# A mixture-of-experts stage: padding rows skipped, the residual gathered and added on VectorE, experts of different groups in turn

## What is computed

```
gi   = argmax(x @ w_rg + b_rg)              # one of 4 groups for each token
le   = (x @ w_re[gi] + b_re[gi])            # 8 experts in the group
top_p, top_i = top_k(softmax(le), 2)        # two of them, both of the same group
gate = p_top * top_p / sum(top_p)
# (token, expert) pairs sorted by expert, each expert padded to blocks of 128 rows
hid  = silu(xb @ w_gate[e]) * (xb @ w_up[e])      # 1024 -> 256
y[token] += gate * (hid @ w_down[e])              # 256 -> 1024
h = h + y
```

## Time and profile before

| | us |
|---|---|
| median of 3 runs | 3121.38 |
| lowest, highest | 3119.2, 3127.32 |
| profiled execution | 3119.75 |
| its span | 3117.8 |

### The profile page before, as it was taken

One profiled execution on the slowest core, in us unless ns is written; L12 is line 12 of the kernel. 1 busy time (PEld: TensorE's weight loads), 2 busy tenths in 40 slices (PEclk: granted clock), 3 DMA queues, 4 the chain that ended last, 5 costly groups with the idle time before them and its releaser, 6 DMA issues. The chain is left out here.

```text
span 3117.8 us, 48627 instructions
## 1 busy us (share of the span) xinstructions
PE 2673.4 (86%) x15109; PEld 2236.8 (72%) x15112; DVE 1747.1 (56%) x3154; ACT 1260.4 (40%) x2369; POOL 724.0 (23%) x923
## 2 busy tenths in 40 slices
PE   5999979997968947998898599799879947989997
PEld 4999958875847836777676488578658836767775
DVE  4222246665755665667765366588733354676664
ACT  3222132225841104556654222288611104675653
POOL 1000023321110002444343143211100002444433
PEclk9999989998988968999999799899979968999998
DMA  6111112215536516899997322222154415999995
GB/s 243 50 56 52 40 60 78 75 65 165 163 121 234 194 61 216 261 301 302 316 281 228 118 87 80 91 83 88 53 198 143 149 39 179 298 359 285 283 308 132
DMA packets 175389, 509.57 MB, mean 163 GB/s; under 512 B 53800, under 2 KB 81456, under 8 KB 150320
## 3 DMA queue, kind: packets, MB, share of 16 engines
q1 hardware_dynamic: 142480, 393.69, 34.7%
q0 software_dynamic: 32800, 114.51, 15.4%
HBM read 374.56 MB, written 133.56 MB: 163 GB/s over the span
## 5 line engine op out<-in xcount | busy, mean ns | idle before, releaser
L1700 DVE TENSOR_TENSOR moe_parts<-expert_w,moe_parts 128x1024 fp32r<-128x1024 f32 x384 | 452.3, 1221 | 238.4 <-ACT moe_parts L1649 234.9
L1582 PE MATMUL ps<-moe_parts,moe_xT 128*128 128x512 f32 x2232 | 551.6, 403 | 23.0 <-issue 16.0
L1582 PEld LDWEIGHTS ps<-moe_parts,moe_xT 128*128 128x128 f32 x2232 | 418.1, 191 | 125.3 <-issue 20.5
L1649 ACT ACTIVATE moe_parts<-expert_w 128x1024 fp32r<-128x1024 f32 x384 | 373.3, 1047 | 80.3 <-PEq L155 78.8
L1109 PE MATMUL ps<-out_w,out_catT 128*128 128x512 f32 x1344 | 322.4, 399 | 14.2 <-DVE out_w L1265 11.8
L560 PE MATMUL ps<-in_gate_w,in_gate_hnT 128*128 128x384 f32 (+1 forms) x1536 | 319.4, 367 | 7.4 <-DVE in_gate_w L679 7.4
L1582 PE MATMUL ps<-moe_parts,moe_hidT 128*128 128x512 f32 x1116 | 289.0, 408 | 26.9 <-DVE moe_hidT L1713 24.2
L560 PEld LDWEIGHTS ps<-in_gate_w,in_gate_hnT 128*128 128x128 f32 x1536 | 278.7, 190 | 37.4 <-issue 7.5
L1109 PEld LDWEIGHTS ps<-out_w,out_catT 128*128 128x128 f32 x1344 | 255.7, 192 | 69.4 <-DVE out_w L1265 12.6
L560 PE MATMUL ps<-in_qk_w,in_qk_hnT 128*128 128x512 f32 x1152 | 268.4, 394 | 9.2 <-DVE in_qk_w L679 9.2
L1582 PEld LDWEIGHTS ps<-moe_parts,moe_hidT 128*128 128x128 f32 x1116 | 205.7, 191 | 76.2 <-DVE moe_hidT L1713 32.8
(11 more groups left out here) (262 smaller groups left out, 4150.8 us busy)
## 6 DMA issues: line engine op xcount, KB each, us to landing
expert_w<-in_w_gate SPq DMA_DIRECT2D x64, 1024.0 KB
expert_w<-in_w_up SPq DMA_DIRECT2D x64, 1024.0 KB
expert_w<-in_w_down SPq DMA_DIRECT2D x64, 1024.0 KB
hn_d<-out_hn SPq DMA_DIRECT2D x32, 512.0 KB, 2.6
in_gate_xt<-in_x SPq DMA_DIRECT2D x16, 512.0 KB
in_qk_xt<-in_x SPq DMA_DIRECT2D x16, 512.0 KB
att_k<-k_d SPq DMA_DIRECT2D x64, 128.0 KB, 2.9
out_ht<-in_x SPq DMA_DIRECT2D x16, 512.0 KB, 4.6
```

The lines of the kernel that those rows point to most:

```text
L1582: last = nc.tensor.matmul(out, left[:, a, k, :], right(b, k), start=(n == 0 and k == 0), stop=(n == 2 and k == K_ - 1))
L1649: nc.scalar.activation(parts[:, j, 0, at], K.expert_w[:, j, at], ACT.Copy).then_inc(w_high.sem, 1)
L1700: nc.vector.tensor_tensor(parts[:, j, 1, at], K.expert_w[:, j, at], parts[:, j, 0, at].bitcast(F32), ALU.subtract).then_inc(w_low.sem, 1)
```

## The change

- Gathers skip rows with an index of T or more. The kernel now uses `K.where` for gathers too, so padding rows are neither read nor written; `K.who`, the spare rows of h and out, and the zeros stored there at the start are gone. xg and a new tile acc are cleared once per phase on GpSimd.
- The accumulating scatter becomes three steps: GpSimd fetches the block's rows of h into acc, VectorE computes z = gate x y + acc in one operation from PSUM (`add`), and GpSimd scatters z with a plain write. ScalarE's `y_scaled` is gone; ScalarE still waits for `lower(m-1)` before it splits the last two pieces.
- `add(m-1)` stands on VectorE between the low part of x and the last two weight pieces. It waits for `lower`, for the fetched rows, and for the scatter before last, of which GpSimd tells it.
- GpSimd's step m: gather(m+2), wait for scatter(m-2), wait for fetch(m-1), copy the index columns, scatter(m-1) when z is there, fetch(m) right behind it.
- The experts are numbered in turn over the groups (expert 0 of group 0, of group 1, ...). A token's two experts are of one group, so two neighbouring blocks share no token, and fetch(m) may run beside scatter(m-1). In `route`, one copy of the logits becomes four, with the columns turned.

```diff
@@ setup
-        zeros = sb("zeros", [P, D])
-            sp.wait_ge(made, 1)
-            for h in K.h_d:
-                sp.dma_start(h[T:T + P, :], zeros[:, :]).then_inc(stored, 16)
             sp.wait_ge(sin_done, 2)
-            sp.wait_ge(stored, 48)
+            sp.wait_ge(stored, 16)
-            own_.link(g.memset(zeros[:, :], 0.0))
@@ route
-            do(V.tensor_copy(le[:, :, :], lg[:, :, GROUPS:NL]))
+            turned_ = le[:, :, :].rearrange("p n (e g) -> p n e g", g=GROUPS)
+            for g in range(GROUPS):
+                own_.mark(V.tensor_copy(turned_[:, :, :, g], lg[:, :, GROUPS + g * EPG:GROUPS + (g + 1) * EPG]))
+            own_.meet()
-            own_.mark(V.tensor_copy(K.who[:, :], found[:, 1, :]))
@@ experts, SyncE
-                load_expert(K, sp, layer, i * 2 + j, j, lambda n: alone(
+                load_expert(K, sp, layer, j * EPG + i, j % 2, lambda n: alone(
@@ experts, GpSimd
-                nc.gpsimd.indirect_dma_start(xg[:, :], None, K.hn_d[layer],
-                                             bass.IndirectOffsetOnAxis(ap=who[:, :], axis=0)).then_inc(gathered_s, 16)
+                g.indirect_dma_start(xg[:, :], None, K.hn_d[layer], bass.IndirectOffsetOnAxis(ap=who[:, :], axis=0),
+                                     bounds_check=T - 1, oob_is_err=False).then_inc(gathered_s, 16)
+            def fetch(m):
+                g.indirect_dma_start(acc[:, :], None, K.h_d[layer], bass.IndirectOffsetOnAxis(ap=at[:, :], axis=0),
+                                     bounds_check=T - 1, oob_is_err=False).then_inc(acc_in, 16)
             def scatter(m):
-                alone(g, y_out, m + 1, K.tick)
-                nc.gpsimd.indirect_dma_start(K.h_d[layer], bass.IndirectOffsetOnAxis(ap=where[:, :], axis=0), y[:, :], None,
-                                             compute_op=ALU.add).then_inc(scattered_s, 16)
+                alone(g, summed, m + 1, K.tick)
+                g.indirect_dma_start(K.h_d[layer], bass.IndirectOffsetOnAxis(ap=where[:, :], axis=0), z[:, :], None,
+                                     bounds_check=T - 1, oob_is_err=False).then_inc(scattered_s, 16)
+            g.memset(xg[:, :], 0.0).then_inc(cleared, 1)
+            g.memset(acc[:, :], 0.0).then_inc(cleared, 1)
+            def step(m):
+                alone(g, x_turned, m + 2, K.tick)
+                g.tensor_copy(who[:, :], column(m + 2)).then_inc(who_set.sem, 1)
+                alone(g, who_set, m + 3, K.tick)
+                gather(m + 2)
+                g.wait_ge(scattered_s, m * 16)
+                g.sem_inc(free, 1)
+                g.wait_ge(acc_in, m * 16)
+                g.tensor_copy(where[:, :], column(m - 1)).then_inc(at_set, 1)
+                g.tensor_copy(at[:, :], column(m)).then_inc(at_set, 1)
+                g.wait_ge(at_set, m * 2 + 1)
+                scatter(m - 1)
+                fetch(m)
@@ experts, ScalarE
-                nc.scalar.activation(y[:, :], yp, ACT.Copy, scale=gate[:, 0:1]).then_inc(y_out.sem, 1)
-                if behind:
-                    y_scaled(m - 1)
                 if ahead:
+                    if behind:
+                        until(a, down, m)
                     split(ni, nj, range(GU_PIECES, PIECES))
@@ experts, VectorE
+            def add(m):
+                until(v, down, m + 1)
+                v.wait_ge(acc_in, m * 16 + 16)
+                v.wait_ge(free, m + 1)
+                nc.vector.scalar_tensor_tensor(z[:, :], yp, K.gates[:, bass.ds(m, 1)], acc[:, :], ALU.mult, ALU.add).then_inc(summed.sem, 1)
                 x_out(m + 1)
+                if behind:
+                    add(m - 1)
                 if ahead:
                     split(ni, nj, range(GU_PIECES, PIECES))
```

More of the change, by code:

```diff
@@ L232, in setup @@
         quarter = sb("quarter", [P, 1])
-        zeros = sb("zeros", [P, D])
-        pos_in, own, tab, sin_done, stored, made = (sem(n) for n in
-            ("pos_in", "own", "tab", "sin_done", "stored", "made"))
+        pos_in, own, tab, sin_done, stored = (sem(n) for n in ("pos_in", "own", "tab", "sin_done", "stored"))
         pool_own = sem("pool_own")
@@ L1042, in step @@
                 alone(sp, added, n + 1, K.tick_sp)
-                sp.dma_start(rows(K.h_d[layer][0:T], n), h2[:, j, :]).then_inc(st, 16)
+                sp.dma_start(rows(K.h_d[layer], n), h2[:, j, :]).then_inc(st, 16)
                 if s.plus(2).within(NT):
@@ L1066, in _ @@
             for e in range(2):
-                load_expert(K, sp, layer, e, e)
+                load_expert(K, sp, layer, e * EPG, e)
             step(s0.plus(1))
@@ L1521, in load @@
             def load(i, j):
-                load_expert(K, sp, layer, i * 2 + j, j, lambda n: alone(
-                    sp, w_low, i * (2 * PIECES) + ((j - 2) * PIECES + (n + 1) * PIECES // 3), K.tick_sp))
-            with sp.Fori(1, NE // 2) as i:
-                for j in range(2):
+                load_expert(K, sp, layer, j * EPG + i, j % 2, lambda n: alone(
+                    sp, w_low, i * (GROUPS * PIECES) + ((j - 2) * PIECES + (n + 1) * PIECES // 3), K.tick_sp))
+            for j in range(2, GROUPS):
+                load(0, j)
+            with sp.Fori(1, EPG) as i:
+                for j in range(GROUPS):
                     load(i, j)
@@ L1559, in _ @@
-            gather(1)
-            until(g, x_turned, 2)
-            gather(2)
+            g.wait_ge(at_set, 1)
+            fetch(0)
+            for m in (1, 2):
+                until(g, x_turned, m)
+                g.tensor_copy(who[:, :], column(m)).then_inc(who_set.sem, 1)
+                until(g, who_set, m + 1)
+                gather(m)
+            def step(m):
[4 more added lines that the diff above has]
+                g.wait_ge(scattered_s, m * 16)
+                g.sem_inc(K.tick, 1)
+                g.sem_inc(free, 1)
+                g.wait_ge(acc_in, m * 16)
+                g.sem_inc(K.tick, 1)
+                g.tensor_copy(where[:, :], column(m - 1)).then_inc(at_set, 1)
+                g.tensor_copy(at[:, :], column(m)).then_inc(at_set, 1)
+                g.wait_ge(at_set, m * 2 + 1)
+                g.sem_inc(K.tick, 1)
+                scatter(m - 1)
+                fetch(m)
@@ L1562, in _ @@
             total = end_of(g, NE)
             with g.Fori(1, total) as m:
-                set_gate(m - 1)
-                alone(g, x_turned, m + 2, K.tick)
-                gather(m + 2)
-                scatter(m - 1)
-            set_gate(total - 1)
+                step(m)
+            g.wait_ge(scattered_s, total * 16)
+            g.sem_inc(K.tick, 1)
+            g.sem_inc(free, 1)
+            g.tensor_copy(where[:, :], column(total - 1)).then_inc(at_set, 1)
+            g.wait_ge(at_set, total * 2)
@@ L1611, in lower @@
                 until(pe, h_low, m + 1)
-                until(pe, y_out, m)
+                until(pe, summed, m)
                 for half in range(2):
@@ L1738, in _ @@
             in_turn(v, first_block, block_)
-            hid_out(end_of(v, NE) - 1)
+            total = end_of(v, NE)
+            hid_out(total - 1)
+            add(total - 1)
 NAMES = ["x", "positions", "norm_mix", "norm_ffn", "w_in_even", "w_out_even", "sgu_norm", "sgu_w", "sgu_b",
```

52 lines of the change are left out of this document (20 added, 32 removed).

## The result

The changed kernel takes 3149.96 us (median of 4 runs, 3149.07 to 3158.80) against 3120.90 for the kernel before on the same chip: ratio 1.0089, 95% interval 1.0072 to 1.0107. It is slower by 29 us (0.9%), where 3080 was forecast. The profiled execution took 3149.97 us, its span is 3148.0.

The account below looks back on a forecast made before the run. Expert loops seen bound by VectorE-TensorE-ScalarE with DMA as full in FF, gathers in Fb. Terms -25.5 - 12 + 2.6 - 6 - 3 + 3.4 - 2 + 1 = -41.5 took 3119.75 to 3078, median 3080 us; range 3040 to 3125.

Parts of the forecast that it names:

- the main risk: Expert loops: the chain add, scatter issue, fetch issue, landing takes 8.8 to 10.3 us, just fitting under TensorE's 9.53 us floor.
- the fetch loop becomes the bound: Rival, expert loops: the chain through the fetch sets the steps; at 11.0 us a round, 3145 us; chance 0.13.
- bF: Steps to an expert's first block behind a second one, nearly all at the floor; late fetches add 2.6 us over 26.
- Fb: Steps to an expert's second block, where TensorE waits for gathered rows; 10.37 to 9.95 us, 28 steps, -12 us.
- FF: Steps opening an expert behind a single-block one, six weight pieces on VectorE; 12.15 to 11.4 us, 34 steps, -25.5 us.
- all hidden: Rival, expert loops: FF at VectorE's 10.8 to 10.9, Fb at 9.55, about -82 us, 3039 us; chance 0.15.
- The bound by DMA time: FF steps: weights plus three indirect transfers ask 11.0 to 12.2 us of DMA, less what weight buffers even out.
- The relief of the queue: Gather and scatter queue: cheaper rows without accumulation take it near 25% of the loop instead of 41%.
- Skipping doesn't skip: Rival, gather and scatter queue: padding rows still make packets, no relief, longer fetch; about -5, 3116 us; chance 0.05.
- Starts: Start of both layers' expert stages: two fills on GpSimd ahead of the first gather, less a shorter gather; +3.4 us.
- End of layer 0: After layer 0's last product: the 8.91 us wait for an empty gather goes, scatter and fetch meet weight loads; -6 us.
- End of layer 1: Last scatters of layer 1: a plain one put 1.5 us shorter than an accumulating one, two in a row; -3 us.

Follow-up runs that it names:

- skip_only: Kernel before, with gather and accumulating scatter skipping padding rows, xg cleared ahead of the first gather, all else as before; 3115.87 us, ratio 0.9973.
- after_start: Changed kernel with only the experts' start reordered: index copy, clearing of xg, first gather, then clearing of acc; 3141.13 us, ratio 1.0055.
- fetch_first: Changed kernel with the fetch of block m issued before the scatter of block m-1, both still after the add; 3202.0 us, ratio 1.0254.
- two_acc: Changed kernel with two buffers for fetched residual rows, fetch(m) issued before add(m-1) is done; 3169.81 us, ratio 1.014.
- no_fetch: Changed kernel without the fetch of residual rows, so the expert stages' residual is left out of the sum; 3063.64 us, ratio 0.9813.
- deep_start: Changed kernel with two acc, z and index buffers, two scatter semaphores, scatter wait one block further back and ahead of the gather, start reordered; 3050.87 us, ratio 0.9762.
- two_two: Changed kernel with two buffers for fetched rows and two for summed rows, add(m) needing the scatter of m-2 landed; 3161.45 us, ratio 1.0137.

## Why the prediction was wrong

**The failed step is the landing in the new wait.** The forecast had the right chain, add - scatter's issue - fetch's issue - landing, and named it as the main risk, but sized it 8.8 to 10.3 us and so found it hidden under 9.53 and 11.4. It measures 11.15. The issues were nearly right: 3.6 us from the add's start to the fetch's issue, against 1.25 + 0.9 + 1.15 = 3.3. The landing is what was missized: 7.6 us against 5.5 plus up to 1.5. The quarter that I took off the gather's 7.4 us for fewer rows isn't there: in `skip_only` the gather lost its padding rows and its landing went from 7.0 to 6.6 us.

**What the forecast left out is what else the add lets go.** It took a gather's landing somewhere in a step and moved it behind the add, where two weight pieces later a weight matrix comes free and a load of 1 MB starts, within 0.1 us of the fetch. In `after_start`, whose trace tells every landing, the 84 fetches of the loops with such a load beside them took 7.6 us on average, the three without one 4.9. A transfer issued 1.5 us ahead of the load is let off (4.5 us in `fetch_first`), and with the loads cut small the fetch takes 4.6 at the same place. With a landing of 4.6 to 4.9 the loop would be 8.2 to 8.5 us, an estimate from these numbers, and would be hidden.

The Trainium skill, "DMA: Bandwidth & Descriptors", section Anatomy of one DMA — SWDGE (gpsimd) path, fits a DMA that GpSimd issues at 2.0 us plus its bytes over 436 KB a microsecond, an estimate of 3.2 us for 512 KB. The trace is near it for the scatter ahead of the load (3.7) and far from it for the fetch beside the load (7.0, both medians).

**A second loop went unseen.** The prediction lets the add wait for the scatter "two blocks back"; in the kernel add(m) waits for the scatter of m-1. That does no harm while the scatter lands in 3.7 us, but it is the loop through z that `fetch_first` and `two_acc` ran into.

**The rival that came true** is the first, "the fetch loop becomes the bound", priced at 3145 us against 3150. Its prices were bF +38 and Fb +18 at 11.0 us a round. By kinds: bF (11.06 - 9.80) x 27 = +34, where +2.6 was forecast; FF (12.19 - 12.03) x 33 = +5, where -25.5 was; Fb (10.08 - 10.29) x 28 = -6, against -12. FF gained nothing, since the add was late there too, which the rival had left at -25.5. That Fb stays under the round of 11.15 us I can only argue: the loop has slack in some steps (the add at 1432.43 waited 1.47 us, the one before 5.55), and which kind pays depends on the step before. The misses inside it, on FF and Fb, cancel, so that its price came so near is luck; its mechanism is what the runs show. With a loop estimate whose upper end was 0.8 above the floor and a row of 7.4 us for the nearest transfer, 0.13 was too little for it.

**FF's gain was real and under-sized.** Where the landing is out of the way, FF is 10.7 (`no_fetch`) and 10.9 (`deep_start`), VectorE's 10.8 of the prediction, not 11.4. The bound by DMA time, 11.0 to 12.2 an FF step, doesn't show above its low end: `deep_start` needs 10.9 with all weights, and the kernel before 12.6 without them. Worth 1.1 us x 33 = 37 us, near the -43 of the "all hidden" rival. The sorting's own slips are small: recounted, FF before is 12.03, not 12.15, and seven of the 28 steps bF stand 0.3 us or more above the floor.

**The relief of the queue came and brought little.** 41.2% to 26.1%, as forecast (near 25%). Rows moved are as forecast too: 256 row transfers more make 1.05 MB, and the queue carries 115.61 MB instead of 114.51. "Skipping doesn't skip" is right that padding rows leave packets and wrong as to their time. In `skip_only` the queue has as many packets as before, 32,800, for 82.05 MB instead of 114.51, and the waits for gathers hardly changed; Fb gained 6 us in the changed kernel instead of 12. The rule of the Trainium skill ("DMA: Bandwidth & Descriptors", section SWDGE vs HWDGE vs iDMA), that an engine takes turns between the two queues at packet boundaries, fits these figures; no run here proves it.

**The smaller terms.** Starts +15, not +3.4: fills and index copies put the gather's issue 2.6 us later, and so behind the first weight load, where its landing doubled (4.5 us before, 9.4 now); I costed the fills and not what they were moved past. End of layer 0 -4.2 against -6: the empty gather still waited 6.71 us, and the add 12.94 for its fetch behind the same load. End of layer 1 -6.7 against -3. Set-up -2.3 against -2. Interleaving 0, as said.

**Why the repair took three loops.** A landing of 7 to 8 us plus GpSimd's 3 us is over one step wherever it stands in a one-step loop: behind the residual buffer (the changed kernel), behind z (`two_acc`), in GpSimd's order (`two_two`). With one or two of them stretched nothing was won; with all three it went at once: -86 us in the loops (1018.2 in `after_start`, 932.6 in `deep_start`).

## What to carry to other kernels

A new transfer into a single buffer closes a loop: consumer, issue, landing, consumer. Ask what else the same consumer lets go: a load that it frees starts when the new transfer does, in every round. Add the loop up with the landing of a transfer issued beside such a load, unshortened, and compare it with the shortest step, not with the mean. If it doesn't fit by a microsecond or two, give it two buffers and look for the same landing in every other wait of the issuing engine, since removing one of several equal loops shows nothing. And an instruction put ahead of a transfer's issue costs also what the transfer then stands behind.

## What the runs showed of the hardware

- A row that the bounds check skips still leaves a small packet: the gather and scatter queue of the changed kernel has 46,192 packets for 115.61 MB, the kernel before 32,800 for 114.51 MB. The difference, 13,392, is what one packet for every slot gives, skipped or not: 283 transfers of 128 rows against 190 are 11,904 slots more, and the 93 new transfers have 16 packets each besides (143 and 144 packets for one of 128 rows). In time the skipped ones are little: in `skip_only` the queue fell to 30.5% of the loop with its packets unchanged.
- The issue of an accumulating scatter takes GpSimd 1.61 us, that of a plain one 1.12 to 1.14 (L1544, 47 and 46 of them). A bounds-checked gather's issue has a mean of 1.30 us in the changed kernel and 1.10 in `no_fetch`, one without the check 1.15 before; the check by itself costs nothing that shows.
- A gather issued 0.13 us behind the first weight load landed after 9.4 us, one issued 1.6 us ahead of it after 4.9.
- In the loops a 512 KB transfer of GpSimd issued some 1.5 us ahead of a 1 MB weight load landed after 3.7 us (scatter, `after_start`) or 4.5 (fetch, `fetch_first`), one issued 0.1 us ahead of it after 7.0 (fetch) or 7.5 (scatter), all medians. In `deep_start` the 29 fetches with no weight load issued from 4 us ahead to 3.5 us behind landed after 3.6 us on average.
